# Seven products of quarter sums for eight in the last gate and up of a float32 two-block model

## The reference

```python
def swiglu(x, w_gate, w_up, w_down):
    return (jax.nn.silu(x @ w_gate) * (x @ w_up)) @ w_down

# second_block, D_FF = 2816
x = x + 0.5 * swiglu(rmsnorm(x, g_ffn1), w1_gate, w1_up, w1_down)
h = rmsnorm(x, g_mix)
...                                   # sparse attention and latent attention on h @ w_in
x = x + concat([out_a, out_b]) @ w_out
x = x + 0.5 * swiglu(rmsnorm(x, g_ffn2), w2_gate, w2_up, w2_down)
return rmsnorm(x, g_final)
```

## Time and profile before

| | |
|---|---|
| median of 3 runs | 1981.02 us |
| the profiled execution | 1978.6 us, span 1976.8 us |
| granted TensorE clock, mean | 0.997 |
| busy: PE / PEld / DVE / ACT / POOL | 96% / 67% / 51% / 32% / 18% of the span |
| split-float matmuls, lines 529 to 531 | 3 x 1240, mean 389 to 393 ns |
| DMA | 422.16 MB, mean 214 GB/s |
| q1 (SP's queue), q0 (GpSimd's) | 51.2%, 11.5% of 16 engines' span |

### The profile page before, as it was taken

How to read it: one execution, slowest core, us unless ns; L and a number is a source line. 1 busy time by engine, 2 the same in 40 slices (tenths; PEclk the granted TensorE clock), 3 DMA queues, 4 the chain that set the end, 5 groups by cost and what they waited for, 6 DMA issues and landing times.

```text
span 1976.8 us, 25018 instructions
## 1 busy us (share of the span) xinstructions
PE 1895.7 (96%) x8777; PEld 1319.3 (67%) x8778; DVE 1008.5 (51%) x1558; ACT 625.0 (32%) x966; POOL 358.5 (18%) x420
## 2 busy tenths in 40 slices
PE   8999999999997799998999999999999899999998
PEld 7888888785332233333688887876656588888786
DVE  5998983444111111111643346866697543334577
ACT  4334435331000000000522225653337642222366
POOL 2012210001211122221033432001146301111200
PEclk9999999999999999999999999999999999999999
DMA  6479972287999999999366896644110032333365
GB/s 216 145 259 273 212 172 86 85 358 304 424 426 426 427 426 423 397 426 418 111 197 213 200 211 193 192 128 120 54 55 12 1 96 86 98 99 100 112 192 170
DMA packets 173032, 422.16 MB, mean 214 GB/s; under 512 B 33932, under 2 KB 91713, under 8 KB 147738
## 3 DMA queue, kind: packets, MB, share of 16 engines
q1 hardware_dynamic: 151386, 366.94, 51.2%
q0 software_dynamic: 21552, 54.17, 11.5%
q10 hardware_dynamic: 16, 0.00, 0.0%
HBM read 411.73 MB, written 65.54 MB: 241 GB/s over the span
## 4 chain that ended last, share of the span: by engine, by line
PE 76%; SPq 8%; DVE 7%; DMA 4%; ACT 3%; issue 2%; POOL 1%; ACTq 0%; DVEq 0%
PE psum L529 15%; PE psum L531 15%; PE psum L530 15%; PE psum L1377 7%; SPq L1243 6%; PE psum L1387 4%; PE psum L1971 3%; PE psum L1973 3%; PE psum L1972 3%; DMA expert_down_third<-in_w_expert_down_dram 2%; DMA arena<-in_w_expert_down_dram 2%; PE psum L670 1%; PE psum L671 1%; PE psum L672 1%; PE psum L2341 1%
## 5 line engine op out<-in xcount | busy, mean ns | idle before, releaser
L529 PE MATMUL psum<-h_hi,w_hi 128*128 128x512 f32 x1240 | 487.4, 393 | 4.6 <-DVE h_lo L1011 1.9
L531 PE MATMUL psum<-h_hi,w_lo 128*128 128x512 f32 x1240 | 482.7, 389 | 0.0
L530 PE MATMUL psum<-h_lo,w_hi 128*128 128x512 f32 x1240 | 482.5, 389 | 0.0
L524 DVE TENSOR_TENSOR w_lo<-w_raw,w_hi 128x1024 fp32r<-128x1024 f32 (+1 forms) x188 | 234.5, 1247 | 435.4 <-ACT w_hi L519 435.3
L519 ACT ACTIVATE w_hi<-w_raw 128x1024 fp32r<-128x1024 f32 (+1 forms) x188 | 198.4, 1055 | 679.8 <-PE psum L531 624.4
L529 PEld LDWEIGHTS psum<-h_hi,w_hi 128*128 128x128 f32 x1240 | 232.9, 188 | 57.4 <-issue 6.3
L530 PEld LDWEIGHTS psum<-h_lo,w_hi 128*128 128x128 f32 x1240 | 233.0, 188 | 49.4 <-issue 1.7
L531 PEld LDWEIGHTS psum<-h_hi,w_lo 128*128 128x128 f32 x1240 | 232.8, 188 | 48.6
L1377 PE MATMUL psum<-arena,w_raw 128*64 128x512 f32 x800 | 181.7, 596 | 13.4 <-DMA arena<-in_w_expert_up_dram 12.6
L1039 DVE SCALAR_TENSOR_TENSOR arena<-arena,vec 128x512 f32<-128x512 f32 x240 | 162.4, 744 | 1.0 <-ACT arena L866 1.0
L1512 ACT ACTIVATE w_raw<-psum 128x256 f32<-128x256 f32 x36 | 13.8, 384 | 461.7 <-PE psum L1377 461.7
(11 more groups left out here) (363 smaller groups left out, 2648.3 us busy)
## 6 DMA issues: line engine op xcount, KB each, us to landing
arena<-in_w_expert_gate_dram SPq DMA_DIRECT2D x44, 1024.0 KB, 23.5
arena<-in_w_expert_up_dram SPq DMA_DIRECT2D x44, 1024.0 KB, 26.1
arena<-in_w_expert_down_dram SPq DMA_DIRECT2D x22, 2048.0 KB, 28.9
weight_terms<-in_w_down_dram POOLq DMA_DIRECT2D x60, 512.0 KB, 6.1
w_raw<-in_w_in_dram SPq DMA_DIRECT2D x44, 512.0 KB, 4.6
w_raw<-in_w_gate_dram SPq DMA_DIRECT2D x88, 256.0 KB, 2.8
w_raw<-in_w_up_dram SPq DMA_DIRECT2D x88, 256.0 KB, 3.0
expert_down_third<-in_w_expert_down_dram SPq DMA_DIRECT2D x10, 2048.0 KB, 28.0
```

Of the source, the lines that this page charges most:

```text
L524: eng.tensor_tensor(wlo[:, s, :, 0:n], raw[:, slot, :, 0:n], whi[:, s, :, 0:n].bitcast(F32), ALU.subtract).then_inc(w_lo, 1)
L529: eng.matmul(o, w_h, x_h, start=first, stop=False)
L530: eng.matmul(o, w_h, x_l, start=False, stop=False)
L531: return eng.matmul(o, w_l, x_h, start=False, stop=last)
```

## The change

Gate and up of the last feed-forward take the same scheme as down: 2 x 2 quarters of tokens (256 each), of the 8 inner tiles, and of the 2816 features (1408 each). The first feed-forward is left as it is, but for the transfers that now stand in it.

- Six super-groups (`N_SG`), five of two feature tiles and one of one tile, each of both gate and up. Each makes seven products in turn, 24 matmuls a chunk as before but with 256 moving columns; 77 chunks instead of 44. `C_DN[1]`, the chunk at which down begins, moves from 230 to 263.
- VectorE adds the seven products up between the splits of weights (`up_sum`, seven for a super-group), scales (`scale_up`), and multiplies (`multiply_up`), four each; ScalarE keeps the first product (`keep`) and takes four silus.
- The tokens' side needs three more operands, made once at the start: full-precision tokens (`full_tokens`), four sums (`sum_operands`), and their high and low parts (`sum_high`, `sum_low`).
- The sums of the gate and up weights, `up_terms`, are made in DRAM by 64 more steps: 32 copies and 32 accumulating ones of 128 x 1408 values. All 160 steps are one numbered row: 108 stand where 48 stood, 4 behind each of the first ten groups of the first feed-forward, 12 behind the eleventh. Four are under way at a time.
- For the last down, GpSimd makes two of the four token sums; the other two (`s1`, `s4`) are two copies and two accumulating transfers within SBUF, behind the last of them.

```diff
-DSLOTS, TERMS = 3, 16 * 4 * N_CH
+DSLOTS = 3
+N_SG = (N_UP + 1) // 2
+N_QUARTER_TERMS, N_UP_TERMS = 8 * N_CH, 64
+STEPS_IN_FIRST, STEPS_PER_GROUP = 108, 4
+ALL_STEPS = 2 * N_QUARTER_TERMS + N_UP_TERMS
...
+        def pe_up(pe):
+            pe.wait_ge(lo_r, 6 * KT + 4)
+            pe.wait_ge(full_r, 4)
+            for g in range(N_SG):
+                for p in range(len(PRODUCTS)):
...
+                    for part in range(up_size(g)):
+                        r = C_UP[1] + up_chunk(g, p, part)
+                        pe.wait_ge(w_lo, r + 1)
+                        for m in range(2):
+                            f = slice(m * P, m * P + P)
+                            for k in range(4):
+                                mm = mm3(pe, o[:, 2 * part + m, :], whi4[:, r % SPLIT, k, f], wlo4[:, r % SPLIT, k, f],
+                                         x_h[:, k, :], x_l[:, k, :], k == 0, k == 3)
+                        mm.then_inc(w_used, 1)
+                        if g == 0 and p == 0 and part == 0:
+                            turn_half(pe, 4, 1, lambda t: group_read(pe, G_MO + 1))
...
-            done = terms_r[n % 2]
-            pool.wait_ge(done, TERMS * j + 16 * (n // 2))
+            done = terms_r[n // 2 % 2]
+            pool.wait_ge(done, 32 * (n // 4))
...
+            else:
+                n -= 2 * N_QUARTER_TERMS
+                step, w, rows = n // 8, n % 8 // 4, slice(P * (n % 4), P * (n % 4) + P)
+                to, source = TERM_STEPS[step]
+                dst = up_terms[w][to][rows, :]
+                src = up_weights(w)[source[0], rows, source[1], :] if isinstance(source, tuple) else up_terms[w][source][rows, :]
+            pool.dma_start(dst, src, accum_op=ALU.add if step >= 4 else ALU.bypass,
+                           max_dma_last_dim=4 * N_UP * P).then_inc(done, 16)
...
+        def pool_sums(pool):
...
+            for n, (total, e) in enumerate(((s1, 0), (s4, 1))):
+                pool.dma_start(total, s2).then_inc(terms_r[n], 16)
+            for n, (total, e) in enumerate(((s1, 0), (s4, 1))):
+                pool.wait_ge(terms_r[n], 16 * (ALL_STEPS // 2) + 16)
+                pool.dma_start(total, act[:, :, e, 0:HALF_T], accum_op=ALU.add).then_inc(terms_r[n], 16)
...
-            if j == 0:
-                for g in range(N_UP - 1):
-                    token_sums(g)
-                    for n in range(5 * g, min(5 * g + 5, 8 * N_CH)):
-                        term_step(pool, 1, n)
+            for g in range(N_UP - 1):
+                token_sums(g)
+                for n in range(STEPS_IN_FIRST + STEPS_PER_GROUP * g, STEPS_IN_FIRST + STEPS_PER_GROUP * (g + 1)):
+                    term_step(pool, n)
             pool.wait_ge(w_lo, C_DN[j] + N_CH)
             token_sums(N_UP - 1)
+            for n in range(STEPS_IN_FIRST + STEPS_PER_GROUP * (N_UP - 1), ALL_STEPS):
+                term_step(pool, n)
...
-            split_lo(dve, C_UP[1], 0)
+            sum_operands(dve, 0)
             residual_rows(dve, 2, 1, C_MO + 8)
+            sum_low(dve, 0)
...
-            pool_ffn(pool, 1)
+            pool_sums(pool)
```

More of the change, by code:

```diff
@@ L1799, in program @@
         first_kept = sem("down_first_product_kept")
+        up_terms = [[nc.dram_tensor(f"up_terms{w}{n}", (4 * P, N_UP * P), F32, kind="Internal").ap() for n in range(4)]
+                    for w in range(2)]
+        full_r = sem("normed_tokens_full")
+        usum_r = sem("up_operand_sums_ready")
+        usum_hi = sem("up_operand_sums_hi")
+        usum_lo = sem("up_operand_sums_lo")
+        up_sum_r = sem("up_products_summed")
+        up_kept = sem("up_first_product_kept")
         joined = sem("down_sums_joined")
@@ new lines, in sum_operands @@
+        def sum_operands(dve, n):
+            first, second, op = ((h_full[:, 0:4, 0, :], full_sum(0), ALU.subtract),
+                                 (full_sum(1), full_sum(0), ALU.add),
+                                 (full_sum(1), h_full[:, 0:4, 0, :], ALU.subtract),
+                                 (full_sum(1), h_full[:, 4:8, 0, :], ALU.subtract))[n]
+            if n < 2:
+                dve.wait_ge(full_r, 4 * n + 4)
+            if n == 1:
+                dve.wait_ge(lo_r, 7 * KT)
+            if n:
+                dve.wait_ge(usum_r, min(n, 2))
+            dve.tensor_tensor(full_sum(n), first, second, op).then_inc(usum_r, 1)
@@ L1865, in sp_ffn @@
                 load_group(1)
-            with sp.Fori(1 - j, N_UP // 2) as i:
-                for g in range(2):
-                    load_group(g, i)
-            load_group(N_UP - 1)
+                with sp.Fori(1, N_UP // 2) as i:
+                    for g in range(2):
+                        load_group(g, i)
+                load_group(N_UP - 1)
+                for done in terms_r:
+                    sp.wait_ge(done, 16 * (N_QUARTER_TERMS // 2))
+            else:
+                sp_up(sp)
             down = down_weights(j)
-            for done in terms_r:
-                sp.wait_ge(done, TERMS * (j + 1))
             for x in range(N_DN):
@@ L2174, in dve_ffn @@
             for x in range(N_DN):
[L2175 to L2176 removed]
+                w_h, w_l, x_h, x_l = down_slots(j, x)
+                if j == 0 and x == 2:
                     scaled(N_UP - 1)
@@ L2611, in act_mix @@
                 if k == 6:
-                    turned_high(act, 6, 0, gain_of("g_ffn2_2"), range(4))
+                    for i in range(4):
+                        turned_high(act, 6, 0, gain_of("g_ffn2_2"), (i,))
+                        full_tokens(act, 0, (i,))
         def dve_mix(dve):
```

415 lines of the change are left out of this document (347 added, 68 removed).

## The result

The changed kernel takes 2014.28 us (median of 4 runs, 2012.51 to 2015.09) against 1981.12 beside it: ratio 1.0166, 95% interval 1.0149 to 1.0184, slower. The prediction said 2006. The profiled execution has a span of 2012.2 us, 35.4 more than before; its mean granted clock is 0.988. TensorE is busy 94% of it, VectorE 55%, GpSimd's queue holds 20.9% of the DMA engines' time with 106.08 MB.

What follows compares the result with a forecast made beforehand. It took TensorE, busy 96% of the span, as the bound. Its terms, -23 + 4 + 6 + 8 + 28 + 4 = +27, on the profiled 1978.6 us gave 2006, range 1965 to 2032 including rivals (own range 1990 to 2022).

Steps and rivals of the forecast that it cites:

- First down stage: +28 said: First feed-forward's down stage: 16 accumulating steps fall into it and delay SP's down weights, +28 us.
- the 5 to 6.5 that it gave as a sign: First down stage: chunks of down weights would land in 5 to 6.5 us between 1200 and 1340.
- Rival 2: First down stage: strict turns, one packet per queue; a chunk per 6.6 us, +49 for +28, 2027 us; chance 0.13.
- Rival 1: First down stage: transfers stay hidden, SP's chunks served as they come, kernel faster, -10, 1969 us; chance 0.28.
- Four under way can't make them faster: GpSimd's transfers: engines are full with two under way, so four only close the gaps between copies.
- the +8 before the experts: Before the experts: added transfers exceed the engines' free time and delay the experts' weights, +8 us (0 to +24).
- Spacing 0.117 said: Last up stage: 1848 products of 256 columns 0.117 us apart, 216.2 us, 23 less (range -40 to -8).
- Rival 3: Last up stage: weight loads don't hide behind 256 columns, 277 us, 38 more than before, total 2067; chance 0.06.
- Feeding: +4 said: Last up stage: VectorE's sums and products between splits overrun some chunks, +4 us in five groups (0 to 10).
- Start: +3.4 and +2.3 said: Last up stage's start: first product later by +3.4 us, chunk 3's split late by +2.3; together +6 (3 to 9).
- The up stage in all: -13 said: Last up stage: matmuls -23, feeding +4 and start +6 us taken together.
- Last down: +4 said: Last down stage: two copies and two accumulating transfers make weight chunks late, +4 us (0 to 12).

Runs made afterwards that it cites:

- 120 steps first: Changed kernel with 120 instead of 108 of the 160 weight-sum steps ahead of the experts: 1998.29 us.
- 12 or 16 in attention: Changed kernel with its last 12 weight-sum steps moved into attention's rotation loop: 1982.19 us; with the last 16, an earlier first split and an earlier third sum: 1974.31 us.
- the early split at the start: Changed kernel with VectorE splitting the last gate and up's first chunk ahead of the residual rows, ScalarE's token high part first: 2009.60 us.

## Why the prediction was right, and where not

The prediction said slower, 2006 us in a range of 1965 to 2032, and 2014.28 was measured: 33 us more than before for the 27 it said. (It added its 27 to the profiled execution's 1978.6 and not to the median of 1981.0.) The direction rests on a mechanism that held: the new accumulating steps reach into the first down stage and make its weights late. The nearness of the number is in good part luck, since larger errors cancelled.

- **First down stage: +28 said, +31 measured, but by errors that cancelled.** Its count of late steps (16), its place and its cause stand (120 steps first; 12 or 16 in attention). The share it gave SP does not: "a queue that is never empty would get one per 1.84 + 2.0 = 3.84 us" was 8.1, and its chunks landed in 27.0 us, not in the 5 to 6.5 that it gave as a sign. Rival 2's mechanism, one packet each in turn, was the right one: three pairs of packet counts bear it out, 1391 and 1351, 2521 and 2441, 1173 and 1227, and so does the order of the single packets. The Trainium skill (DMA: Bandwidth & Descriptors, "SWDGE vs HWDGE vs iDMA") says that an engine takes the queues of the two kinds in turn, and the trace agrees. The prediction had set this rival aside because chunks landed only 2.0 to 2.8 us late in the earlier trace rows, "where strict turns of 16 packets of 4 KB would add 4.8". But the packets there were 5.77 MB / 3006 = 1.9 KB long, 0.774 x 736 / 3006 = 0.19 us each: 16 turns add 3.0, about the 2.0 that was seen in the earlier trace rows. That row did not speak against the rule, and the length stood in it. The window of the earlier trace rows is less clear: 5.73 MB / 1705 = 3.4 KB, 0.729 x 720 / 1705 = 0.31 us, and 16 turns would add 4.9 where 2.8 was seen. There SP moved 2142 packets beside the 1705, so with two steps under way it did not meet one of GpSimd's at each turn; with four, in the same steps, its chunks landed in 10.1 us. Not foreseen either was the clock, which fell to 0.91 over this stage.
- **Rival 2's price of +49 was too high** since it kept GpSimd's work at 68 us of the engines. Accumulating steps with 5 KB packets cost 0.852 x 40 / 6.94 = 4.9 us/MB, 3.5 us each, not 4.25; and with turns they took 16 x 4.15 = 66 us and not 94 or 131. SP lost more per microsecond than the forecast said, for a shorter time. Rival 1 (the transfers stay hidden) is out: its turning point was a chunk per 2.72 us, and one came per 8.1.
- **"Four under way can't make them faster" was wrong**, and with it the +8 before the experts: +1.0. The 108 steps were issued by 391 us; two under way put the gather at 509.9. The error is in the reading that the engines are full, from shares that add up to 1.01 and 1.00: with four under way they added up to 1.07 (82.7% and 23.8%), and a megabyte of accumulating steps took 5.2 us of all engines instead of 5.7 in the same steps, or 5.9 by the earlier trace rows. What it warned of is real, 12 steps further on: +14.6 in the run with 120.
- **Spacing 0.117 said, 0.120 measured.** The bound at which "what 0.227 has over 512/2.4 GHz = 0.2133 is a fixed 0.0134" was the value; the half way between two bounds was not. By 1848 it is 5.5 us. By the 109 ns of the Trainium skill (TensorE: Matmul & The Clock Gate, "Back-to-back issue gap") the stage would have been 201 us; at full clock it measured 221.8. Rival 3 (loads bound the products) is out.
- **Feeding: +4 said.** Waits of this kind were 0.20 to 0.54, 2.4 in all (5.0 less chunk 3's 2.63). What was missed is the last super-group: its third sum stood behind the last split, 4.14 us; moving it gave 4.6 us.
- **Start: +3.4 and +2.3 said, 3.1 and 2.63 measured.** Not foreseen was the clock at half speed behind the gap, 1.4 us (within the 3.2 below).
- **The up stage in all: -13 said (-23 + 4 + 6)**, +0.3 measured (-2.9 + 3.2). Of the 13, 5.5 are spacing, 4.1 the late sum less 1.6 of too much feeding, 3.2 the clock, 2.5 unnamed.
- **Last down: +4 said, +3.0 measured.** In other runs with the same transfers it was -0.5 to +2.2.

So the time came out 8 us above the forecast: by the stages 13 from the up stage and 3 from the first down stage, less 7 before the experts and 1 in the last down.

## What to carry to other kernels

Where a background transfer and a foreground one share DMA engines, compare packets, not bytes or shares. Here each queue got one packet in turn while both had packets waiting, so the foreground is slowed by the length (and kind) of the background's packets; place background transfers by the stage's spare time, or cut their packets. A DMA share near 1 does not show that more transfers under way would bring nothing; only the bytes per microsecond with more under way tell. Waits that late transfers make can cost the clock too, as in the first down stage. And a saving in TensorE's time is only worth what the start, the last group and the clock leave of it: here 23 us of work became 3, and three moved pieces of code made 7 us of gain out of 33 us of loss.

## What the runs showed of the hardware

- While SP's queue and GpSimd's both had packets waiting, the engines took one packet of each in turn: 1391 and 1351 in 40 us.
- An accumulating DRAM transfer took 1.8 times as long for a packet as a copy beside the same load (0.39 and 0.21 us for 5 KB).
- Splitting the packets of 5 KB made two accumulating steps take some 12 us instead of 8.3 beside SP's loads, but let SP's queue through 2.3 times as fast.
- After idle gaps of 3.14 and 4.14 us TensorE's granted clock was 0.50 to 0.60 for the next 3 to 5 us. After the gap of 2.63 us it stayed 1.00 in the changed kernel (1669.21), but was 0.50 for 3.4 us with the early split at the start (1664.7) and for 6.3 us in the run with 16 steps in attention (1634.0), where no gap of 3.14 us stood before it, and for 3.3 us in the run with 12 steps there (1641.9), where one did.
- A GpSimd addition of two SBUF operands, 2816 values a partition, held a VectorE operation of two SBUF operands until it ended: 6.83 us for 1.21.
